# Down products of an MLP in seven-product form, with weight sums made by accumulating DMAs

## The reference, cut to what matters

```python
DEPTH, SEQ, D_MODEL, D_FF = 2, 512, 1024, 4096

def sq_relu_mlp(h, w_up, w_down):
    return jnp.square(jax.nn.relu(h @ w_up)) @ w_down

for i in range(DEPTH):
    ...
    h = rms_norm(x, ln_mlp_pre[i])
    f = sq_relu_mlp(h, mlp_w_up[i], mlp_w_down[i])
    x = x + rms_norm(f, ln_mlp_post[i])
```

## Time and profile before

| | us |
|---|---|
| median of 3 runs (lowest, highest) | 1964.62 (1964.26, 1965.09) |
| profiled execution, from its first to its last instruction (span) | 1962.8 |
| TensorE matmuls busy | 1956.1, x9800 |
| VectorE busy | 1189.4 |
| ScalarE busy | 847.8 |
| GpSimd busy | 12.6 |
| DMA | 188.18 MB, queue of SyncE 29.4% of the 16 engines |

### The profile page before, as it was taken

The page is one execution under the profiler, slowest core; times in us unless marked ns, Lnnn a source line. Parts: engine busy times, 40 slices in busy tenths (PEclk is TensorE's granted clock), DMA queues, the critical chain, the costliest instruction groups (busy, mean ns, idle before and its releaser), DMA issues.

```text
span 1962.8 us, 25307 instructions
## 1 busy us (share of the span) xinstructions
PE 1956.1 (100%) x9800; PEld 1612.3 (82%) x9800; DVE 1189.4 (61%) x1802; ACT 847.8 (43%) x1377; POOL 12.6 (1%) x18
## 2 busy tenths in 40 slices
PE   9999999999999999999999999999999999999999
PEld 8877888888888788888888987777788898888887
DVE  5456654444466765444445686777897647774764
ACT  4534443223246744323223427787434334442431
POOL 0000000000000000000000000000000000000000
PEclk9999999999999999999999999999999999999999
DMA  5222232323233113232422332222232313332331
GB/s 202 86 76 91 71 108 76 118 86 129 80 104 140 44 64 108 86 108 77 138 86 86 108 100 88 82 86 86 86 97 97 129 55 108 97 97 76 118 97 65
DMA packets 51962, 188.18 MB, mean 96 GB/s; under 512 B 5762, under 2 KB 6018, under 8 KB 51204
## 3 DMA queue, kind: packets, MB, share of 16 engines
q1 hardware_dynamic: 51840, 186.56, 29.4%
q10 hardware_dynamic: 4, 0.00, 0.0%
HBM read 184.44 MB, written 2.10 MB: 95 GB/s over the span
## 4 chain that ended last, share of the span: by engine, by line
PE 97%; DVE 1%; ACT 1%; issue 0%; DMA 0%; DVEq 0%
PE ps L399 19%; PE ps L401 19%; PE ps L400 19%; PE ps L428 11%; PE ps L430 10%; PE ps L429 10%; PE ps L452 1%; PE ps L902 1%; PE ps L935 1%; PE ps L916 1%; PE ps L813 1%; PE ps L799 0%; PE ps L784 0%; PE ps L877 0%; PE ps L631 0%; PE ps L659 0%
## 5 line engine op out<-in xcount | busy, mean ns | idle before, releaser
L399 PE MATMUL ps<-HH,WH 128*128 128x512 f32 (+1 forms) x1760 | 651.4, 370 | 0.0
L401 PE MATMUL ps<-HH,WL 128*128 128x512 f32 (+1 forms) x1760 | 646.0, 367 | 0.0
L400 PE MATMUL ps<-HL,WH 128*128 128x512 f32 (+1 forms) x1760 | 645.9, 367 | 0.0
L1069 ACT ACTIVATE WH<-WR 128x1024 fp32r<-128x1024 f32 x305 | 321.4, 1059 | 652.8 <-PE ps L401 374.5
L1687 DVE TENSOR_TENSOR WL<-WR,WH 128x1024 fp32r<-128x1024 f32 x304 | 370.3, 1225 | 189.3 <-ACT WH L1069 182.7
L399 PEld LDWEIGHTS ps<-HH,WH 128*128 128x128 f32 x1760 | 331.8, 189 | 58.4 <-issue 5.2
L401 PEld LDWEIGHTS ps<-HH,WL 128*128 128x128 f32 x1760 | 331.8, 189 | 55.2
L400 PEld LDWEIGHTS ps<-HL,WH 128*128 128x128 f32 x1760 | 332.0, 189 | 52.9
L428 PE MATMUL ps<-WH,HIDH 128*128 128x512 f32 x620 | 241.6, 390 | 0.0
L429 PE MATMUL ps<-WH,HIDL 128*128 128x512 f32 x620 | 241.2, 389 | 0.0
L430 PE MATMUL ps<-WL,HIDH 128*128 128x512 f32 x620 | 241.2, 389 | 0.0
(11 more groups left out here) (261 smaller groups left out, 2019.4 us busy)
## 6 DMA issues: line engine op xcount, KB each, us to landing
WR<-in_up SPq DMA_DIRECT2D x108, 512.0 KB, 3.6
WR<-in_down SPq DMA_DIRECT2D x86, 512.0 KB, 3.5
WR<-in_in SPq DMA_DIRECT2D x56, 512.0 KB, 3.6
WR<-in_swa_in SPq DMA_DIRECT2D x10, 512.0 KB, 4.5
WR<-in_gla_in SPq DMA_DIRECT2D x9, 512.0 KB, 4.8
WR<-in_gla_v SPq DMA_DIRECT2D x8, 512.0 KB, 3.5
WR<-in_gla_g SPq DMA_DIRECT2D x8, 512.0 KB, 4.1
WR<-in_gla_out SPq DMA_DIRECT2D x8, 512.0 KB, 3.6
```

Source lines behind the costliest of these rows:

```text
L399: e.matmul(ps, wh, hi[:, c, cols], start=c == 0, stop=False)
L400: e.matmul(ps, wh, lo[:, c, cols], start=False, stop=False)
L401: y = e.matmul(ps, wl, hi[:, c, cols], start=False, stop=c == x.n - 1)
L1069: e.activation(x.wh[:, 0:n], m.WR[:, u % RAW, 0:n], AF.Copy).then_inc(*k.mark("whi", u))
```

## The change

The 24 down units of the groups are replaced. For a group of 8 down units, let A be the 512 tokens by 1024 hidden channels and B the 1024 by 1024 weights. Both are cut into quarters, A into A11, A12 (first half of the tokens) and A21, A22, B into b11, b12, b21, b22, with signs chosen so that the weight sums are all additions. Seven products of a 256x512 block by a 512x512 block (Winograd's form of Strassen's scheme) stand in for eight:

- t1 = b11 + b12, t2 = t1 + b22, t3 = b12 + b22, t4 = t2 + b21 on the weights' side. Each is made in a raw slot of `WR`: SyncE loads the first quarter there, and a DMA of GpSimd's queue adds the second to what lies in SBUF. t1, t2 and t4 are made one after another in the same slot.
- A11-A21, A21-A22 and two more sums on the hidden side, made by VectorE.
- products b11, b21, t1, b22, t2, t3, t4, each of two units (`STREAM` gives the order of the 14), 12 matmuls a unit.
- the seven results are added up over the groups 0 to 2, each by itself (four in quarters of `MT`, three in the new `PX`); during the last 8 up units seven more additions on VectorE make the four quarters of the result.

A layer's order becomes 8 up units, 14 units of the seven products, three times over, then 8 up units and the 8 plain down units in `t_ends`. The relu moves from VectorE to ScalarE.

```diff
+STREAM = [("b11", 0), ("b21", 0), ("t1", 0), ("b11", 1), ("b21", 1), ("t1", 1), ("b22", 0), ("b22", 1), ("t2", 0), ("t2", 1),
+          ("t3", 0), ("t3", 1), ("t4", 0), ("t4", 1)]
+SEVEN_BANKS = {"b11": 0, "b21": 2, "t1": 4, "b22": 6, "t2": 0, "t3": 2, "t4": 4}
...
+    def raw_slot():
+        r = min(range(RAW), key=lambda r: raw_user[r])
+        return r, raw_user[r] if raw_user[r] >= 0 else None
...
+    def seven(name, quarters):
+        at[name] = u = len(units)
+        chain = [None, None]
+        for what, h in STREAM:
+            q = {n: quarters[j, h] for j, n in enumerate(("b11", "b12", "b21", "b22"))}
+            wh, wl, event = split_slot()
+            if what in ("t2", "t4"):
+                before = u + STREAM.index(("t1" if what == "t2" else "t2", h))
+                add, prior, r = q["b22" if what == "t2" else "b21"], None, chain[h]
+                units.append(Unit(None, DC, wh, wl, event, r, prior, add, ("wlo", before)))
+                continue
+            r, prior = raw_slot()
+            ap = q[{"t1": "b11", "t3": "b12"}.get(what, what)]
+            add = {"t1": q["b12"], "t3": q["b22"]}.get(what)
+            raw_user[r] = len(units)
+            if what == "t1":
+                chain[h] = r
+                raw_user[r] = u + STREAM.index(("t4", h))
+            units.append(Unit(ap, DC, wh, wl, event, r, prior, add, (f"raw{r}", len(units)) if add is not None else None))
...
 def t_mlp(e, k, layer):
-    def downs(o):
-        for q in range(2):
-            u = at[f"down{layer}{o}"] + 4 * q
-            for t in range(4):
-                tokens(e, k, u, 4, m.HIDH, m.HIDL, 8 * (o % 2) + 4 * q, t, 2 * k.bank(), ("mv", u, t),
-                       lambda c: [("hid", layer, 8 * o + c % 8)])
+    def seven(o):
+        u = at[f"seven{layer}{o}"]
+        for j, (what, h) in enumerate(STREAM):
+            x, b, f = k.units[u + j], SEVEN_BANKS[what], SIDE[what]
+            e.wait_ge(*k.on("wlo", u + j))
+            if h == 0:
+                for v in range(2):
+                    e.wait_ge(*k.on(*k.free[b + v]))
+            for v in range(2):
+                for q in range(2):
+                    p, w = 2 * h + q, slice(512 * q, 512 * q + 512)
+                    xh, xl = m.AH[:, p, f, tile(v)], m.AL[:, p, f, tile(v)]
+                    first, last = h == 0 and q == 0, h == 1 and q == 1
+                    e.wait_ge(*k.on("side", layer, 4 * o + p, SIDE_PART[f]))
+                    e.matmul(m.ps[b + v], xh, x.wh[:, w], start=first, stop=False)
+                    e.matmul(m.ps[b + v], xl, x.wh[:, w], start=False, stop=False)
+                    y = e.matmul(m.ps[b + v], xh, x.wl[:, w], start=False, stop=last)
+            y.then_inc(*k.mark("unit", u + j))
...
 def a_cut(e, k, upto):
-        e.wait_ge(*k.on(f"raw{u % RAW}", u))
+        e.wait_ge(*k.on(f"raw{x.raw}" if x.more is None else f"sum{x.raw}", u))
...
 def v_mlp(e, k, layer):
+    def others(p):
+        raw, mix = m.RW[:, p % 2, :, :].rearrange("q c (h f) -> q c h f", h=2), m.SW[:, p % 2, :, :]
...
+        e.tensor_tensor(mix[:, 0:2, :], flat[:, 0:2, :], flat[:, 1:4:2, :], A.subtract).then_inc(*k.mark("mix1", layer, p))
...
+        e.tensor_tensor(mix[:, 2, :], mix[:, 1, :], raw[:, 0, 0, :], A.subtract).then_inc(*k.mark("mix2", layer, p))
...
+        e.tensor_tensor(mix[:, 3, :], mix[:, 2, :], raw[:, 1, 0, :], A.add).then_inc(*k.mark("mixed", layer, p))
...
+    def part(o, what):
+        u = at[f"seven{layer}{o}"] + STREAM.index((what, 1))
+        src, acc = pair(m, SEVEN_BANKS[what]).rearrange("p (a f) -> p a f", a=2), partial(m, what)
+        e.wait_ge(*k.on("unit", u))
+        if o == 0:
+            e.tensor_copy(acc, src).then_inc(*k.mark("part", layer, o, what))
+        else:
...
+            e.tensor_tensor(acc, src, acc, A.add).then_inc(*k.mark("part", layer, o, what))
...
+def g_mlp(e, k, layer):
+    for o in range(3):
+        u = at[f"seven{layer}{o}"]
+        for j in range(14):
+            x = k.units[u + j]
+            if x.more is not None:
+                e.wait_ge(*k.on(*x.sum_of))
+                e.dma_start(m.WR[:, x.raw, :], x.more, accum_op=A.add).then_inc(*k.mark(f"sum{x.raw}", u + j, by=16))
...
 def fetch(e, k, upto):
-        if u >= RAW:
-            e.wait_ge(*k.on("wlo", u - RAW))
-        e.dma_start(m.WR[:, u % RAW, 0:n], k.units[u].ap).then_inc(*k.mark(f"raw{u % RAW}", u, by=16))
+        if x.ap is not None:
+            if x.prior is not None:
+                e.wait_ge(*k.on("wlo", x.prior))
+            e.dma_start(m.WR[:, x.raw, 0:n], x.ap).then_inc(*k.mark(f"raw{x.raw}", u, by=16))
...
-    fetch(e, k, at["down02"] - 1)
-    gains("mix1", 2, ("y", "mlp0", 3))
+    fetch(e, k, at["seven02"] + 8)
+    gains("mix1", 2, ("side", 0, 11, "s"))
```

More of the change, by code:

```diff
@@ L148, in plan, with split_slot @@
     state = {"taken": 0}
+    raw_user = [-1 - RAW + r for r in range(RAW)]
+    def raw_slot():
+        r = min(range(RAW), key=lambda r: raw_user[r])
+        return r, raw_user[r] if raw_user[r] >= 0 else None
+    def split_slot():
+        s = state["taken"] % SPLIT
+        state["taken"] += 1
+        event = ("unit", holds[s]) if holds[s] is not None else None
+        holds[s] = len(units)
+        return m.WH[:, s, :], m.WL[:, s, :], event
     def add(name, tiles, n=DC, extra=None, freed=None):
@@ L171, in plan @@
     for layer in range(2):
[L172 to L179, removed]
+        up, down = each(f"up{layer}", 32), each(f"down{layer}", 8)
+        for o in range(3):
+            add(f"up{layer}{o}", up[8 * o:8 * o + 8])
+            seven(f"seven{layer}{o}", d[f"quart{layer}"][o])
+        add(f"up{layer}3", up[24:])
+        add(f"down{layer}3", down, extra=m.EXTRA["mlp"], freed=("sum7", layer, 6))
         if layer == 0:
@@ L1280, in ups, with mixed @@
+    def mixed(p):
+        e.wait_ge(*k.on("mixed", layer, p))
+        e.activation(m.AH[:, p % 4, 3:7, :], m.SW[:, p % 2, :, :], AF.Copy).then_inc(*k.mark("sideh", layer, p, "s"))
+    def ups(o):
+        u = at[f"up{layer}{o}"]
+        for j in range(8):
             a_cut(e, k, u + j + 3)
             if j:
-                hidden(u + j - 1, i + j - 1)
-        a_cut(e, k, u + n + 3)
-        hidden(u + n - 1, i + n - 1)
-    def downs(o):
-        u = at[f"down{layer}{o}"]
-        a_cut(e, k, u + 7)
-        a_cut(e, k, u + 11)
@@ L1297, in a_mlp @@
+    for o in range(3):
+        ups(o)
+        seven(o)
+    ups(3)
+    a_cut(e, k, at[f"down{layer}3"] + 3)
+    hidden(at[f"up{layer}3"] + 7, 31)
     a_ends(e, k, at[f"down{layer}3"], at["swa_in" if layer == 0 else "glu"], post, then)
@@ L2014, in ups @@
-    def ups(u, i, a, n):
-        for j in range(a, n):
-            v_cut(e, k, u + j + 3)
-            if j:
-                hidden(u + j - 1, i + j - 1)
-        v_cut(e, k, u + n + 3)
-        hidden(u + n - 1, i + n - 1)
-    def downs(o):
-        for q in range(2):
-            u = at[f"down{layer}{o}"] + 4 * q
-            v_cut(e, k, u + 3)
-            for t in range(4):
-                if t == 3:
-                    v_cut(e, k, u + 7)
-                v_rows(e, k, u, 4, t, (u, t), o == 0 and q == 0)
@@ new lines, in ups, with seven @@
+    def ups(o):
+        u = at[f"up{layer}{o}"]
+        for j in range(8):
+            v_cut(e, k, u + j + 3)
+            if o == 3:
+                if j:
+                    plain(24 + j - 1)
+                    together(j - 1)
+                continue
+            if j % 2:
+                first(4 * o + j // 2)
+            if j > 1 and j % 2 == 0:
+                others(4 * o + j // 2 - 1)
+            if j > 2 and j % 2:
+                mixed(4 * o + j // 2 - 1)
+    def seven(o):
+        u = at[f"seven{layer}{o}"]
+        for j in range(14):
+            v_cut(e, k, u + j + 3)
+            if j == 0:
+                others(4 * o + 3)
+            if j == 1:
+                mixed(4 * o + 3)
+            if j and STREAM[j - 1][1]:
+                part(o, STREAM[j - 1][0])
+        part(o, STREAM[13][0])
@@ L2037, in v_mlp @@
+    for o in range(3):
+        ups(o)
+        seven(o)
+    ups(3)
+    v_cut(e, k, at[f"down{layer}3"] + 3)
+    plain(31)
     v_ends(e, k, at[f"down{layer}3"], at["swa_in" if layer == 0 else "glu"], post, then)
@@ L2426, in sync_program @@
     e.dma_start(m.MT[:, :, :], d["bias"]).then_inc(*k.mark("bias", by=16))
-    fetch(e, k, at["down12"] - 1)
-    gains("in2", 4, ("y", "mlp1", 3))
+    fetch(e, k, at["seven12"] + 8)
+    gains("in2", 4, ("side", 1, 11, "s"))
     fetch(e, k, at["qkv"] + 3)
```

161 lines of the change are left out of this document (105 added, 56 removed).

## The result

| | before | after |
|---|---|---|
| median of the runs (lowest, highest), us | 1964.44 (1963.79, 1965.09), 4 runs | 1933.76 (1933.14, 1934.36), 4 runs |
| span of the profiled execution, us | 1962.8 | 1931.7 |

The ratio is 0.9843, with a 95% interval of 0.983 to 0.9857. The change is 30.7 us faster by the medians and 31.1 by the spans; the prediction had 1933.0. The runs of before here were taken beside those of the change, so their median differs by 0.2 us from the one shown first.

A forecast was written before the change was run, and what follows sets the result against it. TensorE, 97% of the chain that ended last, was taken as the bound. Span 1962.8 less 32.6 for 144 matmuls plus 1.0 of stalls gives 1931.2; with 1.8 to the median, 1933.0 us, 8-in-10 range 1929.5 to 1953.

The forecast's parts named there:

- Taken from TensorE, 32.6 us: Six groups of down products: 168 matmuls instead of 192 each, 144 fewer at an unchanged 0.2267 us, saving 32.6 us.
- VectorE and ScalarE hidden: In groups and up units, the added cuts, low parts and additions fit beside TensorE's 2.72 or 5.44 us a unit, costing nothing.
- E = 3.2 us: DMA-engine time of one accumulating DMA, taken as two reads at 1.6 us; possible range 1.4 to 7.9 us.
- The chain of sums: A group's last four sums start at 14.2 us, the last lands at 32.2; unit 13's cut is due by 33.0.
- Stalls, +1.0 us: In group 2 of each layer, gains ahead of unit 10's load delay the sums: 1.3 less 0.8 us spare, twice.
- the sign that I gave of being wrong: Units 11 to 13 of a group starting late behind ScalarE's cuts that wait for a DMA.
- 1962.8 - 32.6 + 1.0 = 1931.2: Whole profiled execution: old span less TensorE's saving plus stalls, 1931.2 us; the 1933 forecast, within 3 us, had 58%.
- the 1.8 us from a span to its own time: Median of the runs lies 1.8 us above the profiled execution's span, making the forecast 1933.0 us.
- Sums late: Rival: sums cost 3.4 to 4.6 us each, delaying each group's end; 1946.4 us at 4; 17% with its second form.
- Its second form: Rival: VectorE's copies out of PSUM in group 0 block GpSimd's descriptor writing, 4.1 us a layer, 1940.2; within the 17%.
- The DMA engines become the bound: Rival at a group's last four sums: from 4.8 us a sum the change loses; up to 2040 us at 7.9; 14%.
- The rate of the matmuls: Rival: 336 added matmuls carrying waits cost 10 ns each, +3.4 us, 1936.4; 7%.

The follow-up runs named there:

- Run 3: Changed kernel with every third matmul of two units a group repeated, so a group has 192 matmuls again, result different: 1964.42 us, ratio 1.0001.
- run 1: Changed kernel without the 48 accumulating DMAs, matmuls, cuts and additions kept, result different: 1931.84 us, ratio 0.9834.
- run 10: Changed kernel with its 14 units reordered (b11 b21 t1 twice, t2 t3, t3 t2, b22 t4 twice) and the gains loaded later: 1942.57 us, ratio 0.9886.
- run 2: Changed kernel with the 48 second DMAs overwriting the slot instead of adding to it, result different: 1931.26 us, ratio 0.9832.
- run 12: The changed kernel as it is, timed again: 1933.70 us, ratio 0.9844.
- Run 6: Changed kernel with the 1 MB of gains loaded later, behind the third of the last up units: 1932.05 us, ratio 0.9836.
- runs 4 and 5: Changed kernel with GpSimd's queue also copying unused weights within HBM after each sum: 256 KB copies 1956.83 us (ratio 0.996), 512 KB copies 1973.17 us (1.0042).
- Run 7: Changed kernel with t3 and b22 changing places in the order of the 14 units: 1942.36 us, ratio 0.9888.

## Why the prediction held, step by step

- **Taken from TensorE, 32.6 us.** Right. 38.08 us a group where 38.1 was forecast, 0.2267 us from start to start, 9656 matmuls. Run 3 shows that it is the count alone, and run 1 (span 1930.0) that 1962.8 - 1930.0 = 32.8 us are there without the sums.
- **VectorE and ScalarE hidden.** Right: with the sums gone (run 1) nothing of them is left on the path. The cut took 1.06 and the low part 1.22 to 1.23 us, as in the earlier trace rows. (ScalarE's 3.4 to 4.0 us an up unit should read 2.95 to 4.0 by its own terms, 1.06 + 3 x 0.63 at the low end, which only adds room.) But the margin was that of one order only. In run 10, with the same work, VectorE's queue passed a late sum on to TensorE's banks.
- **E = 3.2 us.** Measured 2.98, and the reasoning (one more stream at the price of a plain load) is what run 2 shows, 2.98 against 1.61. The high end of 7.9 was far off. The Trainium skill's rule of half the rate (Collectives: The Full Stack, "The bandwidth ceiling: the fold count and why AG ≠ RS ≠ AR"), which the page tells of collectives, comes near here as well: 1.85 times, where it says 2.
- **The chain of sums.** Its start was wrong, its end nearly right, and that is luck. The first of the last four was put at 14.2 us; the six groups have 15.8 to 19.3. I had let unit 10's plain load land 3.6 us after its issue as on free engines, while t2's second sum, and in the groups 2 the gains, were on them; in the last group it took 8.5. The sums themselves then ran faster than 4E says: from the first of the four to the cut of unit 13 it took 14.4 to 17.5 us (959.51 - 944.65 = 14.9 in the last group), where 19.4 - 14.2 + 4 x 3.2 = 18.0 was the forecast. Two errors of opposite sign, 1.6 to 5.1 us too early and 0.5 to 3.6 us too long. The last cut came at 30.5 to 34.1 us, where I had 32.2 for the landing and 33.0 for the limit. A single sum took 5.3 to 13.8 us from issue to landing, 6.9 at the median, where I had said 5 to 7.
- **Stalls, +1.0 us.** Measured 1.7 over the six groups (1.4 in run 12), the same 1.7 in the spans against run 1. The mechanism was right: TensorE waits for `WL` of a late sum's unit, and the sign that I gave of being wrong, a late start behind ScalarE's cuts, shows at unit 13 in this small size (0.81 us of idle time). The place was right in part. I had 0.5 us in each group 2; the profiled execution has 1.25 in one, none in the other, and 0.46 in group 0 of layer 1, for which I had nothing. Run 6 shows that the gains are not the only reason.
- **1962.8 - 32.6 + 1.0 = 1931.2** for the execution stands against 1931.7, and the 1.8 us from a span to its own time held: the profiled execution took 1933.45 us. The median lies 0.3 above that.

The rivals. *Sums late* was the case in kind but not in size: E had to be above 3.4 and is 2.98. Its second form, that VectorE's copies out of PSUM hold up GpSimd's descriptors, can be read off the groups 0, which have these copies, against the groups 1, which have additions in their place. The cut of unit 13 comes at 31.3 and 33.3 against 30.5 and 30.7 us in the change, at 31.2 and 30.5 against 30.9 and 31.3 in run 12, and at 30.3 and 32.4 against 31.2 and 30.9 in run 6: on average 31.5 against 30.9. The 4.9 us of that rival are not there; whether some tenths are, these runs do not tell. *The DMA engines become the bound* is what the runs 4 and 5 bring about on purpose: 0.77 us more behind each sum costs 23 us; 1.3 us costs 39, and the change is lost. My price for it, one us of TensorE for one us of lateness, left out what a longer pause does to the clock, so the point from which the change loses should lie lower than the E = 4.8 that I gave: if a copy is counted as so much more E, 2.98 + 1.3 = 4.3 is beyond it already. No run has sums that are themselves that long. *The rate of the matmuls* did not change. (Its price was mis-stated: 336 matmuls carry waits now and 192 did, so 144 are added, and 10 ns each would be 1.4 us, not 3.4.)

A version that is slightly ahead came out: the change with the gains late, 1932.05 us. Without any late sum this order of units takes 1931.3 to 1931.8 us (runs 2 and 1), so little more can be had from the sums.

## What to carry to other kernels

When work is taken off the bound engine, write down for each transfer in the new, shorter stretch when it may be issued and when it must have landed, with the price of a landing on engines that are shared, not on free ones. Follow each late transfer through the in-order queues behind it, to PSUM banks too: the order of run 10, which looked better for the loads, lost 9 us that way. Run 7's order lost as much by giving other sums less time. A stretch that ends within 1 us of its limit works, but its next user pays: here 256 KB more behind each sum took three quarters of the gain.
